# Another fixed order for the first mixer's four chains of steps

## The chip, the cores and the metric

One NeuronCore of a Trainium2 chip runs the whole program in one launch. The metric is the device time of that launch in microseconds; lower is better. Matmuls are on TensorE (PE), element work on VectorE (DVE), ScalarE (ACT) and GpSimd (POOL), and SyncE (SP) issues the transfers. SBUF is the on-chip memory that all of them read, PSUM the banks that PE writes.

## What is computed

The program is a hybrid block (`first_block`) and then two further layers (`second_block`), on 512 tokens of width 1024. The change touches only the mixer of the first block. From one projection it computes three branches, whose results are joined and projected again:

```python
h = rmsnorm(x, pre_mix_norm[l])
proj = h @ w_in[l]
(a_q, a_k, a_v, s_z, s_xbc, s_dt, g_qkv, g_z, g_b, g_a) = jnp.split(proj, offs, axis=-1)
att = swa_sink_alibi(a_q, a_k, a_v, attn_sinks[l])
ssd = ssd_mixer(s_z, s_xbc, s_dt, ...)       # conv, silu, scan over chunks, gate with silu(z), norm
gdn = gdn_mixer(g_qkv, g_z, g_b, g_a, ...)   # conv, silu, l2norm, triangular solve, scan over chunks
mix = jnp.concatenate([att, ssd, gdn], axis=-1) @ w_out[l]
```

`att` is attention in a window with softmax, `ssd` a state-space scan in 4 tiles of 128 tokens, `gdn` a gated delta rule: per chunk a triangular system is solved by doubling, and then a state is carried over 4 tiles. Its four heads are worked on as two pairs.

## The kernel before

Every engine's program is written by hand. In the first mixer it is a set of Python generators, one per chain, and each `yield` ends a step. The same four chains exist for PE, ACT, DVE and POOL:

- F (`dense`): the projection w_in, 17 feature tiles of 8 steps (one k each, three 128x512 matmuls, L684 to L686, since operands are split in a high and a low part) and then z in 16 longer steps (12 matmuls of 256 columns). On ACT and DVE a tile's end brings its evacuation (L1675), the convolution (three L2327 on DVE) and the silu (L1665, L1667).
- S (`short`): gates; attention in 4 tiles (scores L929, softmax on DVE L2397 to L2408 round four exponentials on ACT, L1719; transposes of the result L943; product with v L954); the state-space scan in 4 tiles (L964 to L1002); at last the gated y is scaled (two L2455, DVE), transposed (L1012, PE) and split (ACT L1756, DVE L2460).
- D and E (`delta(0)`, `delta(1)`): the two pairs of delta-rule heads. Transposes of q, k, v (L1026) and of kn, kb, qn, qe (L1036); decays (L907, DVE L2501, exponential on ACT L1778); the products A and QK (L1049, DVE L2509); five doublings (L1061, L1070 with DVE L2523, L2528, L2531); u and w (L1095, L1102); then for each of 4 tiles wS (L1111, DVE L2553 writes vn), the new state (L1119, DVE L2565 or L2567) and the output o (L1125, L1128, ACT L1796). Tile 0 has no wS: its vn is a plain copy (L2555, SBUF to SBUF). At the end the output is gated and normalised (DVE L2574, L2576, L2578, L2581), transposed (L1136) and written as hH and hL (ACT L1806, DVE L2584).
- G and M: sums of squares of the gated y (DVE L2594, ACT L1815, L1819) and the attention part of hH, hL.

The order in which the steps of the chains stand is one string, `first_order()`, 300 letters long: `walk(IN_ORDER, F=dense(), S=short(), D=delta(0), E=delta(1), G=..., M=...)` takes the next step of the chain that each letter names, and every engine walks the same string (L1147 for PE, L1830 ACT, L2607 DVE, L3197 POOL). An engine does its instructions strictly in that order; semaphores make it wait for the others. An ACT_TABLE_LOAD stands on ACT wherever an activation needs another set of functions than the one loaded (exponential, silu, square root).

POOL makes the low half of each weight chunk, wL = raw - wH (L3099, two instructions of 128x1024 for a chunk), and some of S's products (L3120 to L3147). The chunk after z waits for the last L2594.

Of the kernel before, what the change touches and what calls it, by code (L numbers as in the profile page):

```python
# [256 lines left out]


def first_order():
    return ("FFSFSFFFFFFFFFFFFFFFFFFFFFFFFFFFFDDFSDDFFFFFFFFFDFFFFFFFFSDFFSFSFFFFFFFDSFFFFFDSDFDSDFFFSFDFDFFFFFFSFFFDDFSFFFFFFFDFEESE"  # L260
            "EFFFFEFFFFFFFDSEFFFFFEEFFEESDSFFFFFFFFFFFSDEFFDEEFSFSESFDFEFFESFFFFFFFSFFFEDFEDSFFFSEDESSFFFFSSFSFSSEDESEDEDSSDESFSSGDSD"
            "DSSDDESESSGFFFSGSSEFFFDGEEEDDEDEEDEGSMEDESSEDESDDSEDEESSESDE")


def even_order():
# [13 lines left out]
def build(nc, ins, out):  # L279
# [6 lines left out]
    cum_rows = nc.dram_tensor("cum_rows", (8, 512), F32, kind="Internal").ap()  # L286
    u_rows = nc.dram_tensor("u_rows", (8, 128 * 385), F32, kind="Internal").ap()
    IN_ORDER, EVEN_ORDER, ODD_ORDER = first_order(), even_order(), odd_order()

    ctx = ExitStack()  # L290
# [3378 lines left out]
```

## Time and profile before

| | us |
|---|---|
| median of 3 runs (1781.51 to 1782.4) | 1782.33 |
| the profiled execution | 1781.66 |
| its span | 1780.0 |
| PE busy | 1752.0 (98%) |
| DVE busy | 1154.4 (65%) |
| ACT busy | 783.6 (44%) |
| POOL busy | 659.9 (37%) |

The first mixer's walk takes from about 28 us to 250 us of the span. Times in rows are counted from the span's start. A matmul's end is modelled, so a run of matmuls looks busy through waits of a few tenths of a microsecond. A wait longer than that stands in brackets behind a row, with the instruction that ended it.

### The profile page before, as it was taken

The page shows a single profiled execution, that of the slowest core. Times are in us where ns is not written, and L with a number is a line of the kernel's source. Part 1 is how long each engine was busy: PE and PEld are TensorE (multiplying, and loading weights), DVE is VectorE, ACT ScalarE, POOL GpSimd, SP SyncE. Part 2 cuts the span into 40 slices and gives each one's busy share as a digit, 9 for nine tenths or more (in the row PEclk, how much of TensorE's full clock was granted, in tenths as well). Part 3 has the DMA queues.
Part 4 walks back from the last instruction along what each step waited for, and adds up shares of the span by engine and source line. Part 5 has one row for each costly group of instructions (what it writes and reads, how often), then busy time and mean ns, then how long its engine had stood idle before and what let it go on. Part 6 is the DMA issues. An engine that isn't in the chain of part 4 may idle for free.

```text
span 1780.0 us, 23189 instructions
## 1 busy us (share of the span) xinstructions
PE 1752.0 (98%) x9476; PEld 1447.6 (81%) x9476; DVE 1154.4 (65%) x1565; ACT 783.6 (44%) x1203; POOL 659.9 (37%) x433
## 2 busy tenths in 40 slices
PE   8999989999999999999999999999999999999998
PEld 7788978888888888666798888888888898888886
DVE  5686645333337857867657666689774466666798
ACT  6665345222225644566433433465333244333562
POOL 1444533432553114431244445532101444455431
PEclk9999999999999999999999999999999999999999
DMA  5212032554656534330225555575323245555663
GB/s 201 72 60 73 8 120 87 221 202 177 224 213 224 184 112 137 110 122 25 71 96 189 194 199 192 196 271 171 128 99 118 72 171 188 207 190 202 254 201 107
DMA packets 56549, 270.83 MB, mean 152 GB/s; under 512 B 5578, under 2 KB 11762, under 8 KB 34171
## 3 DMA queue, kind: packets, MB, share of 16 engines
q1 hardware_dynamic: 52090, 264.11, 41.9%
q10 hardware_dynamic: 4352, 5.24, 0.9%
q8 instruction: 75, 1.23, 0.3%
q14 instruction: 32, 0.25, 0.0%
HBM read 232.60 MB, written 38.30 MB: 152 GB/s over the span
## 4 chain that ended last, share of the span: by engine, by line
PE 91%; DVE 4%; ACT 2%; POOL 1%; DMA 1%; issue 1%; SPq 0%; DVEq 0%; ACTq 0%
PE ps L684 26%; PE ps L685 26%; PE ps L686 26%; PE ps L681 1%; PE ps L679 1%; PE ps L680 1%; PE ps L1316 1%; PE ps L1282 1%; POOL wL L3099 1%; PE ps L1275 1%; PE ps L770 1%; PE ps L1269 1%; ACT wH L1613 1%; DMA extra<-w_sums 1%; PE ps L1241 1%
## 5 line engine op out<-in xcount | busy, mean ns | idle before, releaser
L684 PE MATMUL ps<-hH,wH 128*128 128x512 f32 (+1 forms) x1560 | 594.3, 381 | 2.1 <-DVE gT L2327 0.9
L686 PE MATMUL ps<-hH,wL 128*128 128x512 f32 (+1 forms) x1560 | 587.8, 377 | 0.0
L685 PE MATMUL ps<-hL,wH 128*128 128x512 f32 (+1 forms) x1560 | 587.5, 377 | 0.0
L3099 POOL TENSOR_TENSOR wL<-raw,wH 128x1024 fp32r<-128x1024 f32 (+2 forms) x79 | 186.5, 2383 | 423.5 <-ACT wH L1613 416.0
L684 PEld LDWEIGHTS ps<-hH,wH 128*128 128x128 f32 x1560 | 294.1, 189 | 59.6 <-issue 3.4
L686 PEld LDWEIGHTS ps<-hH,wL 128*128 128x128 f32 x1560 | 293.7, 188 | 54.0
L685 PEld LDWEIGHTS ps<-hL,wH 128*128 128x128 f32 x1560 | 294.0, 188 | 51.1 <-issue 0.2
L1613 ACT ACTIVATE wH<-raw 128x1024 fp32r<-128x1024 f32 (+2 forms) x226 | 223.0, 1036 | 151.3 <-PE ps L686 143.6
L2280 DVE TENSOR_TENSOR wL<-raw,wH 128x1024 fp32r<-128x1024 f32 (+1 forms) x147 | 232.7, 1622 | 38.6 <-ACT wH L1613 38.6
L2890 DVE SCALAR_TENSOR_TENSOR ft<-ps,cols,ft 128x511 f32<-128x511 f32 (+1 forms) x176 | 131.6, 748 | 152.1 <-ACT ft L2067 148.9
L2067 ACT ACTIVATE ft<-ps,cols 128x512 f32<-128x512 f32 x88 | 60.6, 689 | 192.0 <-PE ps L686 192.0
L3060 POOL TENSOR_TENSOR extra<-extra 128x512 f32<-128x512 f32 x33 | 44.7, 1353 | 187.9 <-DMA extra<-in_wbig 187.9
L684 PE MATMUL ps<-wH,hH 128*128 128x512 f32 (+2 forms) x320 | 112.4, 351 | 1.7 <-DVE wL L2280 1.5
L686 PE MATMUL ps<-wH,hL 128*128 128x512 f32 (+2 forms) x320 | 109.9, 344 | 0.0
L685 PE MATMUL ps<-wL,hH 128*128 128x512 f32 (+2 forms) x320 | 109.9, 343 | 0.0
L684 PE MATMUL ps<-wH,agH 128*128 128x512 f32 x264 | 103.0, 390 | 1.1 <-DVE wL L2164 1.1
L2669 DVE TENSOR_TENSOR aR<-ft,ps 128x512 f32<-128x512 f32 x22 | 15.1, 687 | 136.2 <-PE ps L686 136.2
L686 PE MATMUL ps<-wH,agL 128*128 128x512 f32 x264 | 102.8, 390 | 0.0
L685 PE MATMUL ps<-wL,agH 128*128 128x512 f32 x264 | 102.8, 389 | 0.0
L3073 POOL TENSOR_TENSOR aR<-aR 128x256 f32<-128x256 f32 x33 | 50.1, 1524 | 94.8 <-DVE agL L2169 94.8
L3052 POOL TENSOR_TENSOR aR<-aR 128x256 f32<-128x256 f32 x33 | 45.2, 1368 | 94.9 <-DVE aR L2899 60.3
L3049 POOL TENSOR_TENSOR aR<-aR 128x256 f32<-128x256 f32 x33 | 43.3, 1311 | 95.6 <-DVE aR L2899 68.0
(430 smaller groups left out, 2847.2 us busy)
## 6 DMA issues: line engine op xcount, KB each, us to landing
raw<-in_wbig SPq DMA_DIRECT2D x114, 1024.0 KB, 5.4
extra<-in_wbig SPq DMA_DIRECT2D x42, 1024.0 KB, 4.8
w_sums<-extra SPq DMA_DIRECT2D x33, 1024.0 KB, 8.7
raw<-w_sums SPq DMA_DIRECT2D x21, 768.0 KB, 6.6
extra<-w_sums SPq DMA_DIRECT2D x15, 768.0 KB, 7.0
rows<-in_rows SPq DMA_DIRECT2D x11, 512.0 KB, 7.9
raw<-in_wbig SPq DMA_DIRECT2D x18, 256.0 KB, 5.2
x<-in_x SPq DMA_DIRECT2D x8, 512.0 KB, 4.8
```

Of the source, the lines that this page charges most:

```text
L684: e.matmul(o, hi, m_hi, start=first, stop=False)
L685: e.matmul(o, hi, m_lo, start=False, stop=False)
L686: return e.matmul(o, lo, m_hi, start=False, stop=end)
L1613: e.activation(wH[r][:, cs], raw[r][:, cs], ACT.Copy).then_inc(*cast.one(c, h))
L2067: e.activation(ft[s][:, :], ps[b0 + t][:, :], ACT.Identity, scale=cols[:, column + 2:column + 3]).then_inc(*ffn.act.one("y", c, t))
L2280: e.tensor_tensor(wL[r][:, cs], raw[r][:, cs], wH[r][:, cs].bitcast(F32), ALU.subtract).then_inc(*low_dve.one(c, h))
L2890: e.scalar_tensor_tensor(y[:, d:512], ps[b0 + t][:, 0:512 - d], cols[:, column + 2 - d:column + 3 - d], y[:, d:512], ALU.mult, ALU.add).th ...
L3049: e.tensor_tensor(aR[:, k, 512:768], aR[:, k, 256:512], aR[:, k, 512:768], ALU.subtract).then_inc(*dn.pool.one(n, "S3", k))
L3052: e.tensor_tensor(aR[:, k, 768:1024], aR[:, k, 1280:1536], aR[:, k, 512:768], ALU.subtract).then_inc(*dn.pool.one(n, "S2", k))
L3060: e.tensor_tensor(b22, b22, b12, ALU.subtract).then_inc(*dn.pool.one(n, "T3", q))
L3073: e.tensor_tensor(aR[:, k, 768:1024], aR[:, k, 1024:1280], aR[:, k, 768:1024], ALU.subtract).then_inc(*dn.pool.one(n, "S4", k))
L3099: e.tensor_tensor(wL[r][:, cs], raw[r][:, cs], wH[r][:, cs].bitcast(F32), ALU.subtract).then_inc(*low_pool.one(c, h))
```

## The change

The string that `first_order()` returns is another one. It has the same number of each letter, so that the same steps run, each chain's in its own order, and only their interleaving differs. No function of the kernel changes.

```diff
 def first_order():
-    return ("FFSFSFFFFFFFFFFFFFFFFFFFFFFFFFFFFDDFSDDFFFFFFFFFDFFFFFFFFSDFFSFSFFFFFFFDSFFFFFDSDFDSDFFFSFDFDFFFFFFSFFFDDFSFFFFFFFDFEESE"
...
+    return ("FFSFSFFFFFFFFFFFFFFFFFFFFFFFFFFFFDDFSDDFFFFFFFFFFDFFFFFFFFSFDFSSDDFFFFFFFSFFFFFSDFSFDDFFFSDFDFFFFFFSFFFDDFESFFFFFFFDFESE"
```

Read against the list of steps, the larger moves are: D's transposes of kb and qn from behind F steps 59 and 64 to behind F 52; E's first transposes (L1026) from F 88 to F 80; E's decays of the first kind (L907) from F 106 to F 114, in one piece with the second; the transposes of attention tile 2 from F 117 to F 114, of tile 3 from F 132 to F 136; D's output for tile 0 from F 146 to F 149. The rest moves by a few places among neighbours. The last 38 letters, behind the last F, order the tail in which no projection step is left.

On ACT the number of table loads in the mixer rises by four, since exponentials and silus alternate more often. Three more places of that kind stand between 125 and 155 us; the first is this one, ACT behind D's two decay exponentials (Dg), where tile 1 of attention (S) and the last convolution tiles of the delta branch (gT_75, gT_76) meet. Rows with + stand only in the changed kernel, rows with - only in the kernel before:

```order
 L1778 ACT_TABLE_LOAD
 L1778 ACTIVATE Dg_128<-Dg_128 128x512 x2
+L1665 ACT_TABLE_LOAD
+L1665 ACTIVATE gT_75<-gT_75 128x512
+L1719 ACT_TABLE_LOAD
 L1719 ACTIVATE S_104,sx_106<-S_104,sx_106 128x256 x4
 L1720 ACTIVATE sx_106<-sx_106 128x4
+L1675 ACTIVATE gT_76<-ps,cols_49 128x512
 L1665 ACT_TABLE_LOAD
-L1665 ACTIVATE gT_75<-gT_75 128x512
-L1675 ACTIVATE gT_76<-ps,cols_49 128x512
 L1665 ACTIVATE gT_76<-gT_76 128x512
```

The silu of gT_75 now stands ahead of attention's exponentials, with a table load before each of the two.

In the tail, on DVE, behind the copy of E's u out of PSUM (uu_105_153): vn_157 is E's vn, Sg_138 and Sg_155 are states of D and of E, vn_139 is D's vn.

```order
 L2544 COPY uu_105_153<-ps 128x512
+L2567 SCALAR_TENSOR_TENSOR Sg_138<-Sg_137,decS_93,ps 64x64 x2
 L2555 COPY vn_157<-uu_105_153 128x128
-L2567 SCALAR_TENSOR_TENSOR Sg_138<-Sg_137,decS_93,ps 64x64 x2
+L2553 TENSOR_TENSOR vn_139<-uu_87_135,ps 128x128
 L2565 COPY Sg_155<-ps 64x64 x2
-L2553 TENSOR_TENSOR vn_139<-uu_87_135,ps 128x128
```

D's state update moves ahead of the copy of E's vn, and D's next vn ahead of E's state.

At the very end of the mixer, on DVE, the scaling of the last y tile (L2455) and E's gate and norm (L2574 to L2581) change places:

```order
 L2460 TENSOR_TENSOR hL_58<-ps,hH_57 128x4x128
-L2455 SCALAR_TENSOR_TENSOR yall_114<-yall_114,gs_94,xd_109 128x256 x2
 L2574 TENSOR_TENSOR ogz_152<-og_151,gz_86 128x512
 L2576 TENSOR_REDUCE rsn_96<-qeT_118 128x4x2
 L2578 RECIPROCAL rsn_96<-rsn_96 128x4x2
 L2581 TENSOR_TENSOR ogz_152<-ogz_152,rsn_96 128x512
+L2455 SCALAR_TENSOR_TENSOR yall_114<-yall_114,gs_94,xd_109 128x256 x2
```

On PE the transposes that wait for them change places in the same way: L1136 of both pairs first, the last L1012 after.

## Rows read from the trace of the kernel before

**Rows 1.** The page: busy time by engine, and the chain that ended last by engine

```profile
PE 1752.0 (98%) x9476; PEld 1447.6 (81%) x9476; DVE 1154.4 (65%) x1565; ACT 783.6 (44%) x1203; POOL 659.9 (37%) x433
PE 91%; DVE 4%; ACT 2%; POOL 1%; DMA 1%; issue 1%; SPq 0%; DVEq 0%; ACTq 0%
```

**Rows 2.** Busy time by stretch: the stretch, its length, busy of each engine, PE clock

```profile
core 0: us, PE busy (x) PEld busy (x) DVE busy (x) ACT busy (x) POOL busy (x), PEclk, DMA share, GB/s
28.00:168.00 140.00, 137.90 (x1016) 114.30 (x1015) 99.95 (x167) 86.94 (x152) 57.76 (x32) 1.00 0.21 72
168.00:228.00 60.00, 59.68 (x778) 56.89 (x777) 34.29 (x76) 24.14 (x43) 32.15 (x30) 1.00 0.08 24
...
244.00:248.00 4.00, 1.43 (x7) 1.43 (x8) 3.48 (x7) 1.58 (x6) 0.00 (x0) 0.54 0.00 0
```

**Rows 3.** PE's waits, 30 to 300 us: us in total, times, longest

```profile
PE ps L1012 <- DVE yall L2455: 3.3, 2, 2.8
...
PE ps L1070 <- DVE P L2523: 0.2, 1, 0.2
```

**Rows 4.** Timeline, 71 to 80 us: start us, us, engine, instruction, count, wait before

```profile
71.46 4.75 POOL L3099 TENSOR_TENSOR wL<-raw,wH 128x1024 fp32r<-128x1024 f32 x2
...
73.91 2.33 DVE L2401 TENSOR_TENSOR sx<-brow,sx 128x4 f32<-128x4 f32 x1
...
77.73 0.60 PE L1036 MATMUL ps<-ident,kb 128*128 128x128 f32 x4
...
79.37 0.63 PE L943 MATMUL ps<-ident,S 128*128 128x128 f32 x4 [1.05 <-DVE S L2408]
```

**Rows 5.** Timeline, 87 to 101 us, ACT, DVE and PE

```profile
89.81 0.63 ACT L1778 ACTIVATE Dg<-Dg 128x512 f32<-128x512 f32 x1 [0.29 <-DVE Dg L2501]
...
91.77 0.51 ACT L1719 ACTIVATE S<-S,sx 128x256 f32<-128x256 f32 x1 [1.33 <-DVE sx L2402]
...
93.96 1.28 ACT L1665 ACT_TABLE_LOAD   x1
...
95.26 0.63 ACT L1665 ACTIVATE gT<-gT 128x512 f32<-128x512 f32 x1
95.53 1.28 DVE L2509 TENSOR_TENSOR AT<-ps,Dg 128x512 f32<-128x512 f32 x2
...
96.73 2.31 DVE L2327 SCALAR_TENSOR_TENSOR gT<-ps,cols,gT 128x511 f32<-128x511 f32 x3
98.61 1.16 PE L1049 MATMUL ps<-qnT,knT 64*128 64x128 f32 x16
...
100.50 1.03 PE L943 MATMUL ps<-ident,S 128*128 128x128 f32 x8
```

**Rows 6.** Timeline, 204 to 209 us, DVE and POOL

```profile
204.64 1.61 DVE L2594 TENSOR_TENSOR yall<-yall,zs 128x512 f32<-128x512 f32 x1
...
207.34 1.03 POOL L3140 TENSOR_TENSOR state<-state,dtot 128x512 f32<-128x512 f32 x1
207.37 1.10 DVE L2555 COPY vn<-uu 128x128 f32<-128x128 f32 x1
```

**Rows 7.** Timeline, 228 to 236 us, the tail's beginning

```profile
228.84 0.69 DVE L2594 TENSOR_TENSOR yall<-yall,zs 128x512 f32<-128x512 f32 x1 [0.19 <-ACT zs L1688]
...
229.61 4.67 POOL L3099 TENSOR_TENSOR wL<-raw,wH 128x1024 fp32r<-128x1024 f32 x2 [4.32 <-DVE yall L2594]
...
230.82 1.23 DVE L2555 COPY vn<-uu 128x128 f32<-128x128 f32 x1
...
231.40 0.28 PE L1119 MATMUL ps<-vn,kd 128*64 128x64 f32 x2
...
231.97 0.58 DVE L2567 SCALAR_TENSOR_TENSOR Sg<-Sg,decS,ps 64x64 f32<-64x64 f32 x2
...
235.53 0.20 DVE L2597 RECIPROCAL gs<-gs 128x8 f32<-128x8 f32 x1 [0.15 <-ACT gs L1819]
```

**Rows 8.** Timeline, 244 to 250 us, PE at the tail's end

```profile
246.57 1.12 PE L1012 MATMUL ps<-ident,yall 128*128 128x128 f32 x4 [2.79 <-DVE yall L2455]
...
249.06 1.11 PE L1136 MATMUL ps<-ident,ogz 128*128 128x128 f32 x4 [0.53 <-DVE ogz L2581]
249.83 0.78 PE L684 MATMUL ps<-wH,hH 128*128 128x512 f32 x1
```

More of the change, by code:

```diff
@@ L259, in first_order @@
 def first_order():
-    return ("FFSFSFFFFFFFFFFFFFFFFFFFFFFFFFFFFDDFSDDFFFFFFFFFDFFFFFFFFSDFFSFSFFFFFFFDSFFFFFDSDFDSDFFFSFDFDFFFFFFSFFFDDFSFFFFFFFDFEESE"
-            "EFFFFEFFFFFFFDSEFFFFFEEFFEESDSFFFFFFFFFFFSDEFFDEEFSFSESFDFEFFESFFFFFFFSFFFEDFEDSFFFSEDESSFFFFSSFSFSSEDESEDEDSSDESFSSGDSD"
-            "DSSDDESESSGFFFSGSSEFFFDGEEEDDEDEEDEGSMEDESSEDESDDSEDEESSESDE")
+    return ("FFSFSFFFFFFFFFFFFFFFFFFFFFFFFFFFFDDFSDDFFFFFFFFFFDFFFFFFFFSFDFSSDDFFFFFFFSFFFFFSDFSFDDFFFSDFDFFFFFFSFFFDDFESFFFFFFFDFESE"
+            "EFFFFEFFFFFFFDSEFFFFFFEEFEFSDFSFFFFFFSEEFFFFFDEDSEFFSDESFFEFFESFFFFFFFFFFDEFSDESFFFSEDESSFFFSSFSFSSDESFSEDEDSEDSFSSDSDED"
+            "SSGDESESGFSFFSGSEDSFFFDGEEDDEDEEEDEGSMEESSDEDSDDSEEDESEESDES")
 def even_order():
```

## Prediction

> **What bounds the kernel now.** I read the page first, then busy time by stretch, then PE's waits, then the timeline at the places that the change moves. The page says PE is busy 98% of the span and carries 91% of the chain that ended last [rows 1]. So a new order of the first mixer can only gain where PE waits inside that mixer. The stretches show how little that is: from 28 to 168 us PE is busy 137.90 of 140 us, from 168 to 228 us 59.68 of 60 [rows 2]. The one place where PE is not the limit is the tail, behind the last projection step at about 228 us. There DVE carries the chain (3.48 us busy of the 4 us from 244, PE 1.43), and PE's clock is down to 0.54 of full in the mean [rows 2]. PE's longest wait of the mixer stands there, 2.8 of 3.3 us, for the scaled y [rows 3]. The tail ends when PE has its last transposes and begins the output projection, at 249.83 [rows 8]. What the change is worth is therefore decided by two things: what it adds to PE's few waits ahead of 228 us, and how long DVE's string of work takes from 228 to 249.
>
> **D's transposes moved to F 52: a small gain.** Ahead of attention's first transposes PE waits 1.05 us, until 79.24 or so, for the softmax [rows 4]. That softmax is paced by POOL: a subtraction of 128x4 numbers on DVE takes 2.33 us there, while POOL's two weight instructions run from 71.46 to 76.21, and ends with them [rows 4]. The new order asks for the scores one F step (about 0.7 us) later, which costs nothing, since DVE then only waits less for POOL. The transposes of qn now stand ahead of this wait, where before they came after it. The group of four like them is 0.60 us with the drain of its last [rows 4]; about 0.45 us of it is issue time. **Minus 0.45 us**, bounds 0 (if the softmax is late by as much) and minus 0.6.
>
> **Four more table loads on ACT: a small loss at one place.** A load takes 1.28 us [rows 5]. Most of the new ones lie where ACT waits anyway. The first pair doesn't. Before, ACT ended D's exponentials at 89.81 + 0.63 = 90.44, and began attention's at 91.77, when DVE had released them [rows 5]. Now a load, the silu of 0.63 us and another load come between: 90.44 + 1.28 + 0.63 + 1.28 = 93.63. Attention's exponentials begin 1.86 us later. DVE waits for them in order, and so does all that is behind it there. The A products ended at 95.53 + 1.28 = 96.81 and now end at about 98.7; PE wants their bank for QK at 98.61, less the 0.45 gained, so 98.16 [rows 5]. **Plus 0.5 us**. The three convolution instructions ended at 96.73 + 2.31 = 99.04, now at 100.9, and the silu of 0.63 us brings 101.55. Before, nobody on PE wanted that tile until F 88. Now E's first transposes stand at F 80, ahead of the L943 that began at 100.50 [rows 5]. PE comes there at about 100.6, some 0.1 later for the two terms above, and the third operand is ready at 101.55. **Plus 0.9 us**. The bounds for both together are 0, if ACT gets a load done earlier than I count it, and plus 1.9, the whole delay. I take 1.4, since both waits are made of measured durations.
>
> By the Trainium skill, page ScalarE: Activation LUTs, section What ACT_TABLE_LOAD costs, a switch of sets costs about 2.66 us, load and drain together. The trace doesn't agree: the load at 93.96 is over at 95.24, and the silu begins at 95.26, so 1.3 us is the whole price here.
>
> **The middle, 100 to 228 us: a hair.** The other moves I followed one by one between the step that releases a PE instruction and that instruction. None of them brings PE to an operand that isn't there by over 0.5 us. E's second doublings (L1070) waited 0.2 us [rows 3] for a result of the step directly before; other steps now stand between. With the 0.32 us that PE is idle in the 60 us from 168 on [rows 2], and as much hidden in modelled ends, **minus 0.5 us**, bounds minus 0.8 and plus 0.8 (one new wait of the size found above). DVE's gating of y tile 0 took 1.61 us at 204.64 and 0.69 us at 228.84, the same instruction [rows 6, 7]; the first overlaps with POOL. In the new order it is behind the products, but it was off PE's path then and is so now: 0.
>
> **The tail: a loss.** DVE copies E's vn (L2555) from SBUF to SBUF. The copy took 1.23 us from 230.82, and 1.10 us for its like at 207.37, where POOL's instruction had begun at 207.34 and ran 1.03 us [rows 6, 7]. Both end when the POOL instruction that was running ends. A state update (L2567, one operand in PSUM) took 0.58 us for two in the midst of POOL's work [rows 7], so that form isn't held up. POOL's two weight instructions ran from 229.61 to 234.28, 2.33 us each, so the first ended at 231.95, and the copy ended just then [rows 7]. In the new order D's state update goes first. It needs PE's L1119, which is done at 231.40 + 0.28 = 231.68 [rows 7]. So it runs from 231.7 to 232.3, and the copy comes to 232.3, a third of a microsecond after POOL's second instruction began. It is then held until about 234.3, against 232.05 before. Of the 2.25 us, 0.6 come back because the state update is already done. Behind the copy hangs E's whole recurrence: its state, its wS, its vn, the next states, and only behind these DVE takes the reciprocal (235.53 before [rows 7]) with which the scaling of y begins. **Plus 1.65 us**, bounds 0 (if the copy still slips in between POOL's two) and plus 2.25. PE had been idle there for tenths and is now for about 2 us, which no cover hides, since no projection step is left.
>
> The Trainium skill, page SBUF — State Buffer, section Who interferes with whom, says that a VectorE copy in a two-port mode and a GpSimd instruction shut each other out for the whole instruction, the first to start going first. The trace agrees, with the 1.23 and 1.10 us; by that rule too the copy at 232.3 waits for 234.3, and it speaks against this change.
>
> **The end of the tail: nothing.** E's gate and norm now stand ahead of the last scaling of y. Before, PE's last two groups of transposes were L1012 at 246.57 and L1136 at 249.06 [rows 8]; now the last is an L1012. DVE has the same instructions ahead of that last group in both orders, and the group is four transposes either way. The output projection needs y only in its second chunk, so the last conversion stays covered. 0, bounds minus 0.8 and plus 0.5.
>
> **Sum.** Minus 0.45, plus 1.4, minus 0.5, plus 1.65, plus 0: 2.1 us. Against the profiled execution, 1781.66 + 2.1 = 1783.8; against the median of 1782.33, 1784.4. I take 1784.0, between the two.
>
> **Rivals.**
> First, the copy slips through, or PE's L1119 is early enough. Then the tail costs nothing and the sum is plus 0.4: 1782.4. For it: the miss is by 0.35 us only, and the 0.45 gained upstream could shift PE against POOL. Against it: POOL's start, E's u and D's L1119 all hang on the same last projection step, so they shift together.
> Second, the new order does gain: the copy is not held, the ACT delays don't reach PE, the end of the tail is 0.8 shorter and the middle gives 0.8 (0.45 + 0.8 + 0.8 = 2.05 us, and up to 0.5 more if PE's clock falls later). That gives 1780.3, at best 1779.8. For it: waits of DVE for POOL, like the 2.33 us and the 1.61 us, are real. Against it: most of them end ahead of a PE that has other work, and the table loads are there.
> Third, slower by more than can be missed: PE's clock. It fell to half (1.2 GHz) after PE had been idle most of the time from 236 on, mean 0.54 from 244 [rows 2]. With a 2 us hole more at 232 it can fall earlier, stay low through the tail and into the output projection. At the low level a group of four transposes took 1.12 us against 0.6 for a like group at the full clock [rows 8, 4], 0.5 us more, and some five such hops lie on the chain behind 236: 2.5 us on top of 2.1, so 1786.9. It decides only if the fall comes before about 240.
> Fourth, by the page's price for a load, 1.4 us more for each, which the trace doesn't bear out: attention's exponentials 2.7 us later still and with them both PE waits, so plus 2.7, 1786.7.
> That the change does not do what it says is no case: the instruction lists of all four engines show the moves.
>
> **Chances and range.** The forecast 0.50, the first rival 0.22, the second 0.12, the third 0.14, the fourth 0.02. What can be told from no change is 0.2%, or 3.6 us. The forecast and the first rival lie within it. Of the second a third could be beyond 1778.8, if the gains were larger than I can find: 0.05 faster. The third and fourth are beyond 1785.9, less the part of the third that stays small: 0.13 slower. The range goes from the second rival's place to the near part of the third, 1780.0 to 1786.6. The forecast's own bounds are 1782.0 to 1785.5.
>
> **What would show it.** In the profile of the changed kernel: L943 at 79 us with a wait of about 0.6 us instead of 1.05; attention's L1719 near 93.6; PE waiting near 98.7 (L1049) and about 0.9 us in E's first L1026 near 101; L2555 in the tail with 2 us instead of 1.23, and PE idle there for as long; the reciprocal L2597 about 1.6 us farther behind the last projection step. If L2555 there is short, the tail term is wrong. If the clock falls before 240, the third rival holds. A different place of PE's work from 28 to 228 us by more than 2 us would say that I followed too few of the moves.

## The result, and the profile after

The changed kernel takes 1787.31 us (median of 7 runs, 1786.14 to 1788.41), the kernel before 1782.33 (7 runs beside them, 1781.11 to 1783.82). The ratio is 1.0025 with a 95% interval from 1.0015 to 1.0034: slower by 5.0 us by the medians, 2.7 to 6.1 by the interval. The prediction was 1784.0 with a range up to 1786.6. It had the sign and two of the mechanisms, and the size is out of its range.

The profiled execution took 1787.66 us, its span 1786.0, against 1781.66 and 1780.0. The page and the busy time by stretch, against [rows 1, 2]:

```profile
PE 1758.4 (98%) x9476; PEld 1452.8 (81%) x9476; DVE 1152.5 (65%) x1565; ACT 788.7 (44%) x1207; POOL 660.3 (37%) x433
...
PE 92%; DVE 4%; ACT 2%; POOL 1%; issue 1%; DMA 0%; SPq 0%; DVEq 0%; ACTq 0%
```

```profile
28.00:168.00 140.00, 137.19 (x1007) 113.58 (x1006) 98.77 (x167) 91.10 (x155) 55.61 (x31) 1.00 0.20 68
168.00:228.00 60.00, 59.92 (x781) 57.09 (x781) 31.81 (x76) 24.00 (x45) 33.68 (x31) 1.00 0.10 35
...
244.00:248.00 4.00, 4.00 (x21) 4.00 (x20) 2.08 (x7) 1.67 (x4) 0.00 (x0) 0.50 0.02 4
```

PE's busy time rose by 6.4 us with the same 9476 instructions. That is no more work but slower work: from 244 to 248 us PE is busy all the time at a clock of 0.50, half of full (1.2 GHz of 2.4), and a group of four transposes (L1012) takes 1.11 us at 243.56, where one took 0.61 at 243.17 before. PE's waits, against [rows 3]:

```profile
PE ps L1136 <- DVE ogz L2581: 3.5, 2, 2.4
PE ps L1119 <- DVE vn L2555: 1.6, 1, 1.6
...
PE ps L943 <- DVE S L2408: 0.7, 1, 0.7
PE ps L1049 <- DVE AT L2509: 0.7, 1, 0.7
PE ps L1026 <- ACT gT L1665: 0.5, 1, 0.5
PE ps L1012 <- DVE yall L2455: 0.4, 1, 0.4
```

The new waits are those that the prediction named: L1119 for the copy of E's vn (L2555), L1049 and L1026 behind ACT's table loads. At the end the wait stands at L1136 instead of L1012, since their order was turned. To see where the time went I compared the same PE instruction in both traces. Three marks say it. At 22 us, in front of the first letter that differs, the changed kernel is already 1.44 us late; executions of the old order show this too (plus 1.37 and plus 1.23 in two of those below), and executions of the new one lack it, so it isn't the change's. At the start of the last matmul of the last z projection it is 1.55 late, so all that the change does ahead of the tail is worth 0.11 us. At the 48th matmul of the output projection it is 6.70 late:

```profile
229.37 0.28 PE L686 MATMUL ps<-wH,hL 128*128 128x256 f32 x1
...
267.92 0.39 PE L686 MATMUL ps<-wH,hL 128*128 128x512 f32 x1
```

From the one to the other it takes 38.55 us, where it took 33.40 (227.82 to 261.22). Behind it the difference stays about the same, 6.79 at 1667 us. Then 0.85 of it comes back, at a place that differs from one execution of a kernel to the next (0.35 in the second execution of the changed one). So the tail and the first matmuls of the output projection hold 5.15 us, all of the loss. I call this distance **the tail's length**; it doesn't depend on what an execution lost ahead of it or behind it, and it carries every comparison below. The tail's beginning, against [rows 7]:

```profile
231.16 4.66 POOL L3099 TENSOR_TENSOR wL<-raw,wH 128x1024 fp32r<-128x1024 f32 x2 [3.71 <-DVE yall L2594]
...
233.27 0.59 DVE L2567 SCALAR_TENSOR_TENSOR Sg<-Sg,decS,ps 64x64 f32<-64x64 f32 x2 [0.94 <-PE ps L1119]
233.90 2.00 DVE L2555 COPY vn<-uu 128x128 f32<-128x128 f32 x1
...
236.05 0.34 PE L1119 MATMUL ps<-vn,kd 128*64 128x64 f32 x4 [1.64 <-DVE vn L2555]
...
239.00 0.20 DVE L2597 RECIPROCAL gs<-gs 128x8 f32<-128x8 f32 x1
```

The copy begins at 233.90, behind POOL's first instruction (231.16 + 2.33 = 233.49), and ends at 235.90 with POOL's second. The reciprocal comes 9.63 us behind the last z projection instead of 7.71: plus 1.92. Now the clock, in stretches of 4 us and around the fall in halves (stretch, length, PE busy, PE's clock, DMA share, GB/s; 1.00 is full clock):

```profile
232.00:236.00 4.00, 2.41 (x26) 1.00 0.00 0
236.00:240.00 4.00, 3.65 (x26) 0.85 0.73 262
240.00:244.00 4.00, 3.73 (x18) 0.50 0.01 2
...
252.00:256.00 4.00, 2.37 (x10) 0.56 0.13 8
256.00:260.00 4.00, 4.00 (x13) 0.59 0.88 358
```

```profile
238.50:239.00 0.50, 0.50 (x5) 0.79 0.93 393
239.00:239.50 0.50, 0.49 (x3) 0.50 1.08 459
```

From 232 to 236 PE was busy 2.41 of 4 us, where it had been 3.88. At about 238.8, 9.4 us behind the last z projection, the clock falls. Before, that was at about 244.3, 16.5 behind it, and full clock was back at 251.1. Here it is back at 249.0, falls again at 252.4 and stays down to 259.3. The end of the tail, against [rows 8]:

```profile
240.27 1.09 PE L1012 MATMUL ps<-ident,yall 128*128 128x128 f32 x4 [0.45 <-DVE yall L2455]
...
253.63 1.11 PE L1136 MATMUL ps<-ident,ogz 128*128 128x128 f32 x4 [2.44 <-DVE ogz L2581]
254.54 1.06 PE L1012 MATMUL ps<-ident,yall 128*128 128x128 f32 x4
255.25 0.78 PE L684 MATMUL ps<-wH,hH 128*128 128x512 f32 x1
```

Reciprocal to first matmul of the output projection is 16.25 us (before 235.53 to 249.83, 14.30): plus 1.95. First to 48th matmul is 12.67 (before 11.39): plus 1.28. With the 1.92 that makes the 5.15. My theory from this: the swap of D's state and E's vn makes POOL hold the copy; the hold costs 1.9 us itself, and the hole that it leaves on PE brings the clock down some 7 us sooner, which costs the other 3.

### The profile page after: what moved, and what is told of

It is laid out like the page before. It is cut to its first block, busy times and chain, and to the rows that moved or that the text cites. A ratio compares the mean times of both kernels' runs of the same rounds, so it can differ in the third digit from the quotient of the medians.

```text
span 1786.0 us, 23193 instructions
## 1 busy us (share of the span) xinstructions
PE 1758.4 (98%) x9476; PEld 1452.8 (81%) x9476; DVE 1152.5 (65%) x1565; ACT 788.7 (44%) x1207; POOL 660.3 (37%) x433
## 3 DMA queue, kind: packets, MB, share of 16 engines
q8 instruction: 75, 1.23, 0.3%
## 4 chain that ended last, share of the span: by engine, by line
PE 92%; DVE 4%; ACT 2%; POOL 1%; issue 1%; DMA 0%; SPq 0%; DVEq 0%; ACTq 0%
PE ps L684 26%; PE ps L685 26%; PE ps L686 26%; PE ps L681 1%; PE ps L679 1%; PE ps L680 1%; PE ps L1316 1%; PE ps L1282 1%; POOL wL L3099 1%; PE ps L1275 1%; PE ps L770 1%; PE ps L1269 1%; ACT wH L1613 1%; PE ps L1061 1%; PE ps L1070 1%
```

## Experiments

"Before" is the kernel before, run beside each. All tail numbers are read as above, in us; "fall" is where the half clock begins, counted from the last z projection, and "reciprocal" and "projection" (the first matmul of the output projection) likewise. Each row is one execution.

| kernel | copy | reciprocal | fall | projection | tail's length |
|---|---|---|---|---|---|
| before | 1.23 | 7.71 | 16.5 | 22.01 | 33.40 |
| before, second execution | 1.23 | 7.71 | 16.3 | 22.01 | 33.31 |
| changed | 2.00 | 9.63 | 9.4 | 25.88 | 38.55 |
| changed, second execution | 2.01 | 9.63 | 9.5 | 25.87 | 38.56 |
| swap alone | 2.00 | 10.87 | 6.6 | 27.30 | 39.61 |
| swap alone, second execution | 2.00 | 10.77 | 6.8 | 27.21 | 39.61 |
| changed, vn from PSUM | 0.29 | 7.93 | 17.7 | 22.29 | 34.09 |
| changed, POOL waits | 0.23 | 7.93 | 17.6 | 22.29 | 34.10 |
| changed, old tail | 1.23 | 7.72 | 16.5 | 22.01 | 33.38 |
| swap alone, hole filled | 2.02 | 9.71 | 19.9 | 24.01 | 36.08 |
| changed, hole filled | 2.02 | 9.67 | 19.5 | 24.03 | 35.90 |
| changed, all gaps filled | 2.03 | 9.65 | none | 23.53 | 34.30 |
| before, all gaps filled | 1.22 | 7.71 | none | 22.48 | 33.24 |
| end swaps alone | 1.22 | 7.72 | 9.4 | 23.61 | 35.72 |
| end swaps alone, second execution | 1.23 | 7.72 | 16.9 | 22.07 | 33.60 |
| early moves alone | 1.23 | 7.71 | 19.1 | 22.01 | 34.66 |
| before, vn from PSUM | 0.29 | 7.71 | 16.8 | 22.01 | 33.54 |
| before, vn from PSUM, gaps filled | 0.29 | 7.72 | none | 21.94 | 32.72 |

### Which part of the order costs

**The swap alone**, in the order of before:

```diff
-            "DSSDDESESSGFFFSGSSEFFFDGEEEDDEDEEDEGSMEDESSEDESDDSEDEESSESDE")
+            "DSSDDESESSGFFFSGSSEFFFDGEEDDEEDEEDEGSMEDESSEDESDDSEDEESSESDE")
```

> The kernel before with one piece of the change alone: in the tail, D's state 1 and o 1 stand ahead of E's first vn (the letters EDD become DDE), nothing else. Theory: the copy then begins a third of a microsecond after GpSimd's second weight instruction and is held to its end, 1.2 becomes 2.0 us, the reciprocal comes 1.5 to 2 us later, and the clock falls before 240 instead of at 244; together 3.5 to 5.2 us slower than before: 1786 to 1787.5. Rival A (the clock's earlier fall needs the other swaps too): 1.5 to 2 us slower, 1784.1. Rival B (the copy slips in between GpSimd's two, and the loss is elsewhere): within 0.5 us of before.

Measured: 1787.28 against 1782.67, ratio 1.0029 (1.0019 to 1.0038). Three letters of 300 cost what the whole change costs.

```profile
229.47 4.65 POOL L3099 TENSOR_TENSOR wL<-raw,wH 128x1024 fp32r<-128x1024 f32 x2 [4.33 <-DVE yall L2594]
...
231.57 0.59 DVE L2567 SCALAR_TENSOR_TENSOR Sg<-Sg,decS,ps 64x64 f32<-64x64 f32 x2 [0.94 <-PE ps L1119]
232.20 2.00 DVE L2555 COPY vn<-uu 128x128 f32<-128x128 f32 x1
```

The copy ends at 234.20 with POOL's second instruction (229.47 + 4.65 = 234.12). The reciprocal is 3.2 us late rather than the 1.5 to 2 of the theory, since here the clock falls so early (at about 234.3) that E's recurrence ahead of it runs at half clock too. The theory stands, and both rivals are out. The tail is even 1.06 us longer than in the changed kernel (39.61 against 38.55), whose clock falls later (9.4 against 6.6). Which of the other letters in the tail does that, no run shows.

**The old tail on the new order**: the changed kernel, with the letters from 262 on taken from the kernel before.

> The changed kernel with the last 39 letters of the order taken from the kernel before (all from D's wS 1 on); everything up to there stays new. Theory: what the change does ahead of the tail is worth plus 0.1 us by the marks on TensorE, so the time is that of the kernel before, 1782.0 to 1783.0, and the copy takes 1.0 to 1.3 us again. Rival (the two ACT table loads and the moves in the middle cost, as the sum of the prediction had it with plus 0.45): 1782.8 and up, to 1784 if the traces hid some of it. Rival B (the shifted arrival at the tail holds the copy even in the old order): 1786 to 1787.

Measured: 1783.12 against 1782.67, ratio 1.0004 (0.9995 to 1.0013), tail's length 33.38. The median lies between the theory's range and the first rival's, and only the marks tell them apart. All that stands ahead of the tail costs 0.2 us by the marks (1.30 late at the start, 1.49 at the last z projection). So the loss is in the tail's letters, and among them in the swap.

**The early moves alone**: the order of before, with letters 49 to 117 from the new one (one execution).

> The kernel before with the part of the new order up to E's first transposes alone (letters 48 to 116: D's transposes of qn and those of the softmax's surroundings earlier, four more table loads on ScalarE, E's first transposes at F 80); from there on the old order. The prediction had minus 0.45 for the softmax wait and plus 1.4 for the two waits of TensorE behind the table loads: plus 0.95 by the last projection step, less what this run's input transfers shift at the very start. Theory from the new kernel's waits (0.7 at the softmax, 0.7 at QK, 0.8 at E's first transposes, against 1.05, 0 and 0): plus 0.9, and the middle gave back 0.8 of it in the changed kernel, whose sum was plus 0.1. Rival (the waits were there before too, in other instructions): plus 0.1 already here, and the middle is worth nothing.

Measured: 1.38 late at the start and 2.49 at the last z projection, so plus 1.11 us from these moves. PE's waits up to 230 us are those of the changed kernel:

```profile
PE ps L943 <- DVE S L2408: 0.7, 1, 0.7
PE ps L1049 <- DVE AT L2509: 0.7, 1, 0.7
PE ps L1026 <- ACT gT L1665: 0.5, 1, 0.5
PE ps L1070 <- DVE P L2523: 0.2, 1, 0.2
```

The changed kernel has plus 0.11 to 0.20 there (seven executions of it and of its variants with edits in the tail only). So the middle of the new order, from E's transposes to the last z projection, gains 0.9 to 1.0 us. It comes in small pieces. At places where both orders have done the same steps, and with what each execution was late at 22 us taken off, the changed kernel is 1.12 us late at 114 us (times of the kernel before), 0.82 at 143, 0.53 at 164 and 0.14 at 223; the order with the early moves alone stays at 1.10. Its last row, L1070's wait, isn't in the changed kernel's list. The rival, plus 0.1 already here, is out.

**The swaps at the end of the tail alone**: the order of before, with letters 279 to 300 from the new one. It was profiled in two executions, since the first had an odd clock.

> The kernel before with the last 22 letters of the order from the changed kernel: D's o 2 and E's o 2 later, E's gate and norm ahead of the last scaling of y, the last group on TensorE one of y. The copy stays where it was. The prediction had 0 for this, from minus 0.8 to plus 0.5. The first and third runs differ by little else and by 34.1 against 33.4 us from the last projection step to product 28. Theory: plus 0.7 us in that distance, 34.1, and 1783.2 in time. Rival A (the prediction's 0): 33.2 to 33.6. Rival B (they gain 1 us, as the changed kernel is 1.1 us shorter there than the bare swap): 32.4.

> The same program as in the seventh run once more, for one look. There the granted clock fell at 237.0 us, though TensorE had done up to 236 us what it does in the kernel before, whose clock fell at 244.3; the distance from the last projection step to product 28 was 35.7 us, but the median of eleven times was only 0.5 us above before. Theory (where the clock falls differs from one execution to the next, when TensorE's work is near what is wanted): another place now, 243 us or later, and a distance of 33.8 to 34.3 us. Rival (the order at the end of the tail fixes the early fall): 237 again and 35.7 us.

Measured: 1783.34 against 1782.88, ratio 1.0002 (0.9993 to 1.0011). The two executions of this one program differ. The first:

```profile
232.00:236.00 4.00, 3.56 (x31) 1.00 0.25 33
236.00:240.00 4.00, 3.39 (x18) 0.62 0.55 231
```

The second:

```profile
232.00:236.00 4.00, 3.89 (x44) 1.00 0.00 0
236.00:240.00 4.00, 2.95 (x23) 1.00 0.75 264
```

(The second began all of its tail 1.6 us later, so the same stretch holds a little other work.) The clock fell 9.4 us behind the last z projection in the first, 16.9 in the second, and the tail's length was 35.72 and 33.60. The median sides with the second. So these swaps cost 0.2 us (33.60 against 33.40), not the 0.7 that I expected. Of the 0.7 of the PSUM kernel below, 0.2 stands already at the reciprocal (7.93 against 7.71), and 0.4 in the first 48 matmuls of the output projection (11.80 against 11.39): the clock fell at 17.7 there and came back only at 24.5, behind the projection's start. And where the clock falls isn't given by the program alone. That made second executions of the others necessary (below).

### What holds the copy

**The copy from PSUM**, in the changed kernel:

```diff
-                        e.tensor_copy(vn[p][:, :, :], uu2[p][:, :, i, :]).then_inc(*gdn[p].dve.one("v", i))
+                        e.tensor_copy(vn[p][:, :, :], ps[b][:, :].rearrange("p (h i d) -> p h i d", i=4, h=2)[:, :, i, :]).then_inc(*gdn[p].dve.one("v", i))
```

> The changed kernel with one edit: VectorE takes the first vn of each delta chain from PSUM (where u still stands) instead of from its copy in SBUF, so this instruction has one operand outside SBUF, as the state update has that was not held up. The order stays the new one. Theory (the copy, held by GpSimd's second weight instruction, makes a hole on TensorE, and the hole brings TensorE's clock down before 240 us, so that the tail and the start of the output projection run at half clock): the copy in the tail takes 0.2 to 0.4 us instead of 2.0, the distance from the last projection step to the reciprocal falls from 9.6 to about 7.7 us or less, the clock falls at 242 or later, and the time is 4 to 5 us below the changed kernel's, about as the kernel before: 1781.8 to 1783.3. Rival A (only the hold costs, the clock is a matter of the new order at the tail's end): 1.5 to 2 us come back, 1785.4. Rival B (the loss lies in other moves, upstream or at the tail's end): no change, 1787.

Measured: 1784.01 against 1782.67, ratio 1.0007 (0.9998 to 1.0016). The copy takes 0.29 us in the midst of POOL's instruction, the reciprocal is at 7.93, the clock falls at 17.7, and the tail is 34.09 us long: 4.46 of the 5.15 are back. The median is above the 1781.8 to 1783.3 expected, by the 0.7 that the tail keeps.

**POOL's second instruction behind the copy**, in the changed kernel, the copy reading SBUF as it did:

```diff
-                    w.wait_ge(*cast.at(c, h))
+                    w.wait_ge(*cast.at(c, h)); w.wait_ge(*(gdn[1].dve.at("v", 0) if (c, h) == (C_Z + 2, 1) else cast.at(c, h)))
```

> The changed kernel with one more wait: GpSimd begins its second weight instruction of the tail only when VectorE has done E's first vn. The copy reads SBUF as before, the order is the new one. Theory (GpSimd's running instruction is what holds the copy): the copy takes 0.2 to 0.4 us, or up to 0.6 if it still overlaps the end of GpSimd's first; GpSimd's second begins behind it, near 234.3; the reciprocal comes 7.7 to 8.0 us behind the last projection step, the clock falls after 242, and the distance from that step to product 28 is 34.1 us as in the first run (38.6 in the changed kernel): 1783 to 1784.2. Rival A (the copy is slow for another reason, its tiles in SBUF): it takes 1 to 2 us still, and the time stays 1787. Rival B (GpSimd's later end holds other VectorE instructions instead, of the scaling of y): 35 to 37 us.

Measured: 1784.00 against 1782.88, ratio 1.0006 (0.9997 to 1.0015).

```profile
231.15 2.35 POOL L3099 TENSOR_TENSOR wL<-raw,wH 128x1024 fp32r<-128x1024 f32 x1 [3.71 <-DVE yall L2594]
...
233.88 0.23 DVE L2555 COPY vn<-uu 128x128 f32<-128x128 f32 x1
...
234.25 2.35 POOL L3099 TENSOR_TENSOR wL<-raw,wH 128x1024 fp32r<-128x1024 f32 x1 [0.75 <-DVE vn L2555]
...
237.29 0.20 DVE L2597 RECIPROCAL gs<-gs 128x8 f32<-128x8 f32 x1
```

The same copy with the same operands takes 0.23 us when POOL does nothing, 2.00 when POOL's second instruction runs. Both remedies give the same tail (34.09 and 34.10). That POOL's running instruction holds the copy is shown from both sides, and also that this hold is what the loss hangs on.

The Trainium skill, page SBUF — State Buffer, section Who interferes with whom, says that a VectorE instruction with at most one SBUF input and outside the two-port modes doesn't contend with GpSimd, and that with one in a two-port mode, as a copy can be, whoever issues first blocks the other for the whole instruction. No trace shows the mode, but the times agree: 0.29 us from PSUM, 2.00 us from SBUF behind GpSimd's start, 0.23 us from SBUF with GpSimd's start behind it.

**The copy from PSUM in the old order**: the same edit on the kernel before.

> The kernel before with the one edit of the first run: the first vn of each chain taken from PSUM. The order is the old one. Theory: the copy takes 0.3 us instead of 1.2, the state update behind it comes 0.5 to 0.9 us earlier and with it the reciprocal, if ScalarE's sum is there by then: the distance from the last projection step to product 28 is 32.6 to 33.0 us against 33.4, the time 0.4 to 0.8 us below before: 1782.1. Rival A (ScalarE's table load ahead of the square root of the sums, which ends 0.15 us ahead of the reciprocal, is what the reciprocal waits for): 33.3 to 33.4, no change. The clock may fall at another place than at 244 us; then the distance is up to 2.3 us longer with the copy at 0.3 us all the same.

Measured: 1782.11 against 1782.73, ratio 1.0000 (0.9991 to 1.0009). The theory's 0.4 to 0.8 us didn't come; rival A holds:

```profile
232.57 0.29 DVE L2555 COPY vn<-ps 128x128 f32<-128x128 f32 x1
...
235.65 1.28 ACT L1819 ACT_TABLE_LOAD   x1
...
236.95 0.30 ACT L1819 ACTIVATE gs<-gs,cols 128x8 f32<-128x8 f32 x1
237.28 0.20 DVE L2597 RECIPROCAL gs<-gs 128x8 f32<-128x8 f32 x1
```

The copy is 0.9 us shorter, yet the reciprocal stays at 7.71 (237.28 less 229.57). It waits for ACT's square root behind a table load. So in the kernel before the copy's 1.2 us lay beside other work; only when it grew to 2.0 and came later did it reach the path.

### The clock

**Gaps filled in the changed kernel.** The extra transposes multiply the identity into a PSUM bank that nobody reads before the next product clears it:

```diff
+            def keep_warm(n):
+                clear(1)
+                for _ in range(n):
+                    e.transpose(ps[1][:, 0:128], ident[:, :], ident[:, :])
...
+                    keep_warm((6, 2, 1, 0)[i])
...
+                        if p == 1:
+                            keep_warm((12, 1, 0)[i])
...
+                keep_warm((10, 14)[p])
```

> The changed kernel with transposes of the identity into a free PSUM bank put where TensorE waits in the tail, which do nothing but keep it busy: 12 ahead of E's first state (behind which the copy is waited for), 1 ahead of E's second, 6, 2 and 1 ahead of the groups of y 0 to 2, 10 and 14 ahead of the last groups of D and E. No result depends on them. Theory: the hold on the copy stays (2.0 us, reciprocal 9.3 to 9.7 us behind the last projection step), but the granted clock stays full through the tail and the start of the output projection, and 2.5 to 3.5 us come back: 1783.8 to 1784.8. Rival A (the clock doesn't matter, the chain of DVE does): no change, 1787. Rival B (the idle of TensorE isn't filled well enough): the clock still falls, later; 0.5 to 2 us come back.

Measured: 1783.28 against 1782.67, ratio 1.0003 (0.9995 to 1.0012). The copy is held as before (2.03 us, reciprocal at 9.65), the clock stays at 1.00 through every stretch from 228 to 260, and the tail is 34.30 us long, 4.25 shorter than in the changed kernel. That is more than the 2.5 to 3.5 expected, since the half clock of the kernel before goes as well. Rival A, that the clock doesn't matter, is out.

**Gaps filled in the kernel before**, with 5, 2, 0, 20 transposes ahead of the y groups, 1 and 7 ahead of E's states 1 and 2, 9 ahead of E's o 3 and 6 ahead of E's last group:

> The kernel before, in its own order, with transposes of the identity into a free bank where TensorE waits in the tail (1 and 7 ahead of E's states 1 and 2, 9 ahead of E's o 3, 5, 2 and 20 ahead of the groups of y 0, 1 and 3, 6 ahead of E's last group). Nothing depends on them. Theory (half clock costs on the chain, in the kernel before as well): the granted clock stays full from 228 to 260 us, the transposes of four and the first matmuls of the output projection take their full-clock times (0.6 us and 0.23 us apart), and the distance from the last projection step to product 28 falls from 33.4 us to 31 to 32; 1780.3 to 1781.7. Rival A (the half clock of the kernel before hides behind VectorE's chain): 33.0 us or more, no change in time. Rival B (the extra transposes get in the way of real ones): 33.5 to 35 us, slower by up to 1.5 us.

Measured: 1783.01 against 1782.88, ratio 0.9999 (0.9990 to 1.0008), tail's length 33.24. A miss: the length is rival A's, and rival B's delay is in it. The seven ahead of E's state 2 got in the way (that state began 11.25 us behind the last z projection, not 10.34), the full clock gave 1.1 us back from there to the 48th matmul, and the two cancel.

**Both remedies in the old order**, the copy from PSUM and fillers, fewer than in the last run (2 instead of the 7):

> The kernel before, in its own order, with both remedies: E's and D's first vn taken from PSUM as in the first run, and transposes of the identity where TensorE waits, fewer than in the fifth run where they delayed E's state 2 (2 instead of 7 there; 3, 2 and 20 ahead of the groups of y 0, 1 and 3; 8 ahead of E's o 3; 6 ahead of E's last group). Theory: no hold (minus 0.5 to 0.9 on VectorE's chain), full clock from 228 to 260 us (minus 1.0, what the fifth run gave back against the 0.9 that its fillers cost at E's state 2), so the distance from the last projection step to product 28 is 31.5 to 32.3 us against 33.4, and the time 1 to 2 us below before: 1780.8 to 1782.0. Rival (the hold isn't on the path in the old order, or other fillers get in the way): 32.6 to 33.4 us, no change in time.

Measured: 1782.24 against 1782.73, ratio 0.9996 (0.9987 to 1.0005), tail's length 32.72, 0.68 shorter than before. This is the shortest tail of all, but in the time it can't be told from the kernel before. The theory had 31.5 to 32.3; it was wrong to count the hold, as the copy from PSUM in the old order shows. The rest adds up: E's state 2 began 10.71 us behind the last z projection, 0.37 later than before, and from there to the 48th matmul it took 22.01 us against 23.06. That is 1.05 us from the full clock, as in the run above, less 0.37 for two fillers.

**Only the copy's hole filled.** 16 transposes ahead of E's first state, once on the bare swap and once on the changed kernel (`keep_busy` is the same loop of transposes as `keep_warm`):

```diff
...
-                        clear(a)
+                        clear(a); keep_busy(p * (16, 0, 0)[i])
                         w.wait_ge(*gdn[p].pool.at("kd"))
```

> The kernel before with the swap of D's state and E's first vn alone (as in the second run), and 16 transposes of the identity ahead of E's first state, so that TensorE is busy for about 2 us just where the held copy made it wait; nowhere else. The copy is held as before. Theory (the hole at the copy itself brings the clock down early): the clock stays full until 242 us or later; the distance from the last projection step to product 28, 33.4 us before and 39.6 with the bare swap, becomes 33.4 + 1.9 = 35.3 (34.9 to 35.9), and the time that of before plus 2: 1784 to 1785.2. Rival A (the later gaps of TensorE bring it down anyway, since everything is late): the clock falls before 240 again, 38 us or more, 1787.

> The changed kernel with 16 transposes of the identity into a free bank ahead of E's first state, just where the held copy made TensorE wait, nothing else; the sixth run's edit on the changed kernel. Nothing depends on them. The copy stays held (2.0 us). Theory (the hole brings the clock down early): the fall comes behind 243 us, the distance from the last projection step to product 28 is 35.7 to 36.5 us against 38.6 in the changed kernel, and the median 2 to 3 us below the changed kernel's, 2.2 to 3 us above before: 1785 to 1785.8. Rival (the clock falls early by chance or by the whole tail's idle): median within 0.7 us of the changed kernel's 5.0 above before: 1787 to 1788.

Measured: the first 1785.28 against 1782.88, ratio 1.0014 (1.0005 to 1.0023); the second 1785.57 against 1782.60, ratio 1.0018 (1.0009 to 1.0027). The copy takes 2.02 us in both and the reciprocal is 2.0 late, so the hold is whole. The first is a little above what was expected (36.08 us against at most 35.9), the second inside. In the second:

```profile
232.00:236.00 4.00, 3.99 (x35) 1.00 0.20 43
236.00:240.00 4.00, 2.96 (x24) 1.00 0.55 225
240.00:244.00 4.00, 3.09 (x24) 1.00 0.00 0
```

With 3.99 instead of 2.41 us of work from 232 to 236 the clock stays at 1.00 up to 19.5 us behind the last z projection. This shortens the tail of the bare swap by 3.53 us (39.61 to 36.08) and that of the changed kernel by 2.65 (38.55 to 35.90). By medians the loss against before falls from 4.6 to 2.4 and from 5.0 to 3.0. Nothing downstream was filled. So the hole at the copy, not the idle time behind it, is what brings the clock down early. Of the 2.5 to 2.7 us of tail that stay, 2.0 are the hold (projection at 24.01 and 24.03 against 22.01) and 0.5 to 0.7 lie in the first 48 matmuls, where the late fall's half clock still holds.

**Second executions.** Since the clock can fall at two places in one and the same program, the changed kernel, the bare swap and the kernel before were profiled once more.

> The changed kernel once more, for a second look. Theory (a held copy makes a hole that brings the clock down before 240 us every time or nearly so): copy 2.0 us, clock at half before 240.5 us, distance from the last projection step to product 28 37.5 us or more. Rival (the early fall was one draw): clock at half first behind 243 us, distance 35.5 to 36.3 us, which is 33.6 plus 1.9 for the hold and up to 0.8 for a late rise.

> The kernel before with the swap of D's state and E's first vn alone, for a second look. Theory: copy 2.0 us, the clock falls between 234 and 240.5 us again, distance 37.5 us or more. Rival: it falls behind 243 us, distance 35.3 to 36.3 us.

> The kernel before once more, for a second look. Theory (without a held copy the clock mostly stays up until 243 to 249 us): distance 33.3 to 34.7 us. Rival (without the hole it falls before 240 about as often): 35 us or more.

Measured: all three as the theory has it, and close to the first executions (table). With the copy held for 2.0 us and an open hole the early fall came in four executions of four; without that hold, and without fillers, in one of nine (the end swaps' first execution, whose cause stays open); with the hold but the hole alone filled in none of two. The second execution of the changed kernel, in stretches:

```profile
232.00:236.00 4.00, 2.36 (x22) 1.00 0.19 37
236.00:240.00 4.00, 3.38 (x22) 0.67 0.58 227
240.00:244.00 4.00, 4.00 (x22) 0.50 0.02 4
```

## Why the prediction missed

**D's transposes ahead of the softmax** (minus 0.45): right. L943 waits 0.71 instead of 1.05 us, minus 0.34.

**Four more table loads** (plus 0.5 and plus 0.9): right in mechanism and sum. The chain on ACT in the changed kernel is the one that I added up, with the loads at 1.28 and no drain behind them:

```profile
92.02 1.28 ACT L1665 ACT_TABLE_LOAD   x1
93.31 0.63 ACT L1665 ACTIVATE gT<-gT 128x512 f32<-128x512 f32 x1
93.97 1.28 ACT L1719 ACT_TABLE_LOAD   x1
95.26 0.51 ACT L1719 ACTIVATE S<-S,sx 128x256 f32<-128x256 f32 x1
...
100.45 1.16 PE L1049 MATMUL ps<-qnT,knT 64*128 64x128 f32 x16 [0.68 <-DVE AT L2509]
...
103.24 0.33 PE L1026 MATMUL ps<-ident,gT 128*128 128x128 f32 x1 [0.52 <-ACT gT L1665]
```

PE waits 0.68 and 0.52; by the marks each of the two places costs 0.75 us, where the prediction had 0.5 and 0.9. With the softmax's gain the early moves came to plus 1.11 where the prediction had plus 0.95.

**The middle** (minus 0.5, bounds minus 0.8 and plus 0.8): the sign was right, the size was minus 0.9 to minus 1.0, past the bound. That brings the part ahead of the tail to plus 0.1 or 0.2, against the 0.45 predicted. The prediction found no place for the gain. The marks spread it over several small steps between 114 and 228 us; the wait at L1070 is 0.2 of it, and what the rest is made of stays open.

**The tail's hold** (plus 1.65): right. The copy took 2.00 us, and the reciprocal came 1.92 later. The mechanism was shown from both sides.

**The swaps at the tail's end** (0): plus 0.2 on the old order, inside the bounds.

**The clock** was the step that failed. The sum took the tail's hole at its own length and left everything behind it at the durations of before. The third rival said what would really happen, with the condition "before about 240" (it was 238.8) and 2.5 us as the price (about 3.0: 5.15 less 1.92 less 0.2), and its time of 1786.9 is 0.4 from the median. It got a chance of 0.14 and so no part in the forecast and little in the range. What the prediction had in hand was enough for more: PE's clock was already down to 0.54 in this same tail [rows 2], its cause was named as PE's idle time there, and the term of 1.65 us was 1.65 us more of idle time, ahead of the place where the clock fell. They were weighed as rivals, the hold alone at 0.50 and the hold with the clock at 0.14, when given the hold the early fall was likely: four of four. One reading misled here: the prediction has PE idle "most of the time from 236 on" ahead of the fall, but PE was busy 2.70 of 4 us from 236 to 240 and 2.71 from 240 to 244, and the fall at 244.3 came half a microsecond into its wait of 2.79 us. The fall did not need an engine that was idle for long. The range was short for the same reason: its upper end, 1786.6, stood in front of the rival's own 1786.9.

The test put down in the prediction, "if the clock falls before 240, the third rival holds", read the trace rightly.

## What to carry to other kernels

When a change adds a wait to PE in a stretch where its clock is already near falling, price the wait and the clock as one case: here a hold of 1.9 us cost 5, and filling the hole with idle transposes, which did nothing about the hold, took back 2 to 3.5. A VectorE copy within SBUF that began beside a running GpSimd instruction ended here with it (2.00, 1.23 and 1.10 us, against 0.23 alone); look at where it starts against GpSimd's boundaries before moving it by one place, or let it read PSUM. Filling isn't free either: seven transposes ahead of a state whose operand was there put it 0.9 us back. And compare two executions of one kernel before reading a clock difference as an effect of the order: the same program had its fall at 9.4 and at 16.9 us, 2.1 us apart in the tail's length.

## What the runs showed of the hardware that I had not expected

The half clock outlasts its cause. In the changed kernel PE is busy 4.00 of 4 us from 244 to 248, and the clock stays at 0.50 until 249.0. A late fall isn't harmless either: in the kernel with the early moves alone it fell 19.1 us behind the last z projection and rose at 26.0, so that the output projection, which began at 22.01, ran its first matmuls at half clock, and the tail was 1.26 us longer than before (34.66 against 33.40) though every step up to its beginning was on time. An execution with the fall at 16.5 and the rise at 23.3 pays less. By this, differences of up to 1.3 us between two of these kernels can come from the clock's place alone, without an early fall.

The copy from PSUM took 0.29 us while POOL was in the midst of its instruction, with the same 128x128 elements that took 2.00 from SBUF.
